# A merged attention and delta-rule stage: moved reductions, one more copy on ScalarE, doubled output buffers, and a mask that becomes a limit

## The reference

```python
# head group A, per block of 128 queries
s = einsum(qn, k_nope) + einsum(qp, k_pe)          # scaled
s = where(k_pos <= q_pos, s, -inf)
o = softmax(s) @ v
# head group B, per chunk and head (g is the cumulated log decay of the chunk)
decay = exp(where(causal, g[:, None] - g[None, :], -inf))
lower = where(strict, (k_beta @ k.T) * decay, 0)
sol   = triangular_solve(lower + eye, [v_beta, k_beta * exp(g)])
a_qk  = where(causal, (q @ k.T) * decay, 0)
# then a scan over chunks that carries a state of 128 x 128 per head
```

## Time and profile before

| | |
|---|---|
| median of 3 runs | 2444.69 us (2444.61 to 2447.8) |
| the profiled execution | 2443.78 us |
| its span | 2442.0 us |
| TensorE busy, whole span | 2187.7 us |
| VectorE, ScalarE, GpSimd busy, whole span | 1028.3, 839.1, 652.5 us |
| merged stage, first instruction of TensorE | 691.58 us |
| output stage, first of TensorE | 1502.00 us |

### The profile page before, as it was taken

The page is one execution under the profiler, slowest core; times in us unless marked ns, Lnnn a source line. Parts: engine busy times, 40 slices in busy tenths (PEclk is TensorE's granted clock), DMA queues, the critical chain, the costliest instruction groups (busy, mean ns, idle before and its releaser), DMA issues. The chain is left out here.

```text
span 2442.0 us, 35600 instructions
## 1 busy us (share of the span) xinstructions
PE 2187.7 (90%) x11479; PEld 1242.1 (51%) x11480; DVE 1028.3 (42%) x2282; ACT 839.1 (34%) x2043; POOL 652.5 (27%) x1122
## 2 busy tenths in 40 slices
PE   5999999999967898899889996999948999999990
PEld 2545455545434565666656673455534444444440
DVE  2334243333345576666677663243451222222223
ACT  2264363552644454454544551111111111111113
POOL 1000001000034534624633501333322222222224
PEclk9999999999988999999999997999968999999995
DMA  9212121121252333434244218533305888999777
GB/s 344 80 61 76 48 76 57 45 76 61 85 171 78 111 122 121 146 107 139 77 135 143 70 53 316 185 123 131 112 26 154 225 246 267 303 324 294 220 220 299
DMA packets 221897, 361.77 MB, mean 148 GB/s; under 512 B 45579, under 2 KB 143526, under 8 KB 218294
## 3 DMA queue, kind: packets, MB, share of 16 engines
q1 hardware_dynamic: 207926, 309.57, 37.2%
q0 software_dynamic: 13824, 50.34, 8.6%
HBM read 259.93 MB, written 99.93 MB: 147 GB/s over the span
## 5 line engine op out<-in xcount | busy, mean ns | idle before, releaser
L704 PE MATMUL pV<-keys_values_then_all,w_in_sb 128*128 128x512 f32 x768 | 341.5, 598 | 4.1 <-DVE keys_values_then_all L518 4.1
L2170 PE MATMUL hidden_ps<-w,keys_values_then_all 128*128 x752 | 332.5, 595 | 1.7 <-SPq L2042 1.7
L1234 ACT ACTIVATE probs<-scores,neg_max 128x512 f32<-128x512 f32 (+3 forms) x320 | 196.3, 620 | 302.4 <-DVE neg_max L1343 182.1
L2170 PEld LDWEIGHTS hidden_ps<-w,keys_values_then_all 128*128 128x128 f32 x752 | 143.5, 191 | 182.8 <-issue 182.8
L704 PEld LDWEIGHTS pV<-keys_values_then_all,w_in_sb 128*128 128x128 f32 x768 | 145.0, 191 | 177.8 <-issue 177.0
L1808 PE MATMUL out_ps<-keys_values_then_all 128*128 128x512 f32 x512 | 226.8, 601 | 2.8 <-ACT keys_values_then_all L1657 2.8
L1496 PE MATMUL scores<-ident,probs 128*128 128x128 f32 x1088 | 155.9, 285 | 39.8 <-ACT probs L1234 39.1
L2100 ACT ACTIVATE keys_values_then_all<-hidden_ps 128x256 f32<-128x256 f32 x47 | 18.0, 383 | 457.0 <-PE hidden_ps L2170 457.0
L2180 PE MATMUL expert_ps<-w_sb,keys_values_then_all 128*128 x368 | 169.8, 604 | 0.0
L1808 PEld LDWEIGHTS out_ps<-keys_values_then_all 128*128 128x128 f32 x512 | 97.1, 192 | 122.5 <-issue 116.7
L1496 PEld LDWEIGHTS scores<-ident,probs 128*128 128x128 f32 x1088 | 120.3, 143 | 69.7 <-ACT probs L1234 60.9
(11 more groups left out here) (370 smaller groups left out, 3310.3 us busy)
## 6 DMA issues: line engine op xcount, KB each, us to landing
w<-in_w_dram SPq DMA_DIRECT2D x64, 1024.0 KB, 10.2
w_sb<-in_w_dram SPq DMA_DIRECT2D x32, 1024.0 KB, 14.2
keys_values_then_all<-in_x_dram SPq DMA_DIRECT2D x32, 512.0 KB, 5.4
w_mod_rows<-in_w_mod_dram SPq DMA_DIRECT2D x16, 1024.0 KB, 4.9
keys_values_then_all<-in_w_mod_dram SPq DMA_DIRECT2D x4, 2048.0 KB, 14.9
qkv_d<-l_out SPq DMA_DIRECT2D x32, 256.0 KB, 2.3
keys_values_then_all<-y_d SPq DMA_DIRECT2D x16, 512.0 KB, 4.7
x_d<-keys_values_then_all SPq DMA_DIRECT2D x16, 512.0 KB, 2.8
```

Of the source, the lines that this page charges most:

```text
L704: last = pe.matmul(pV[n % 2][:], win[:, k, QKV0 + c * P:QKV0 + (c + 1) * P], hT[:, s % 2, k, :], start=(k == 0), stop=(k == ND - 1))
L1234: act.activation(prob[:, e, 0:w].rearrange("p t k -> p (t k)"), pS[e][:, 0:w * P], ACT.Exp, scale=-1.0, bias=nmin[:, i % 2, h, b:b + 1], a ...
L2170: last = pe.matmul(pH[par][:], xT[par][:, k], m.w13[:, ds(slot, 1), k].rearrange("p s n -> p (s n)"), start=(k == 0), stop=(k == ND - 1))
```

## The change

- `X j+1` of heads 2 and 3 is put directly behind those of heads 0 and 1, behind the scores and ahead of `V j`; before, they stood between the halves of `V j`.
- The transposed probabilities of head 1 are copied by ScalarE too: three copies there, one on VectorE.
- One of the two `O` turns of a quad goes behind `V`.
- `A` comes at the end of the second quad of a tile in every case, and `AS` behind the minima of the tile's last quad, or, where the tile before has fewer than four key tiles, in the next tile's first quad; the last ones are put by hand.
- `G` and `O2` are held back until the next `V`, or until the next `K` or `QS`.
- GpSimd's multiplication by the triangle is gone. Instead VectorE's `G` is a subtraction followed by a minimum with a tile `future` (zero in the triangle, -1e30 outside), and `K` and `KA` read the exponential straight from `dm`.
- `A_ahead` and `qk_ahead` have two buffers each, by the parity of the chunk.
- SyncE loads the next decay rows behind the stores of `KA` in place of behind `K`, and several loads of the stage's start (keys and queries, gate, bias, modulation weights) go behind the first stores.

```diff
-        if i and o < AH // 4:
-            for hp in (2 * o, 2 * o + 1):
-                atoms.append((0.13 * (TILE[i - 1] // 4 + 1), [("O", i - 1, hp)]))
+        if i > 1 and first and TILE[i - 1] < 4:
+            atoms.append((0.0, [("AS", i - 2, 0)]))
+        turns = [(0.13 * (TILE[i - 1] // 4 + 1), [("O", i - 1, hp)]) for hp in (2 * o, 2 * o + 1)] * (i > 0 and o < AH // 4)
+        atoms += turns[:1]
         if ahead:
-            atoms.append((0.8 * ahead, [("S", j + 1), ("X", j + 1, 0), ("X", j + 1, 1)]))
-        if i and last:
-            atoms.append((0.0, [("A", i - 1, 0)] * (TILE[i] < 4) + [("AS", i - 1, 0)]))
-        atoms.append((0.65 * n, [("V", j, 0)] + [("X", j + 1, 2), ("X", j + 1, 3)] * (ahead > 0) + [("V", j, 1)]))
-        if i and o == AH // 4 - 1 and TILE[i] >= 4:
+            atoms.append((0.8 * ahead, [("S", j + 1)] + [("X", j + 1, e) for e in range(4)]))
+        if i and last and TILE[i] >= 4:
+            atoms.append((0.0, [("AS", i - 1, 0)]))
+        atoms.append((0.65 * n, [("V", j, 0), ("V", j, 1)]))
+        atoms += turns[1:]
+        if i and o == AH // 4 - 1:
             atoms.append((0.0, [("A", i - 1, 0)]))
...
-    atoms.append((0.0, [("BX", NT - 1, 0), ("B2", NT - 1, 0)]))
+    atoms.append((0.0, [("AS", NT - 2, 0), ("BX", NT - 1, 0), ("B2", NT - 1, 0)]))
...
+    held = []
     for cost, step in steps:
+        if step[0] in ("O2", "G"):
+            held.append(step)
+            continue
+        if step[0] in ("K", "QS"):
+            order += held
+            held = []
         order.append(step)
         owed += cost * share
         while atoms and owed >= atoms[0][0]:
             owed -= atoms[0][0]
-            order += atoms.pop(0)[1]
+            order += atoms[0][1]
+            if atoms.pop(0)[1][0][0] == "V":
+                order += held
+                held = []
+    order += held
...
@@ sync
-            load_kk(2)
-            load_q(1)
-            load_gate(0)
-            ...
-            load_mod(0)
+            def load_next():
+                ...   # the same loads
...
-                    if n + 2 < NT:
-                        wait(em_ready, n + 1)
-                        load_g(n + 2)
                 elif kind == "KA":
                     store_products(n)
+                    if n + 2 < NT:
+                        load_g(n + 2)
+                    if n == 0:
+                        load_next()
...
@@ gpsimd
+            pool.memset(future[:], 0.0).then_inc(limit_made, 1)
+            pool.wait_ge(limit_made, 1)
+            pool.affine_select(out=future[:], in_=future[:], compare_op=ALU.is_ge, fill=NEG, base=0,
+                               pattern=[[1, P]], channel_multiplier=-1).then_inc(limit_made, 1)
...
-                if kind == "G":
-                    wait(exp_ready, n + 1)
-                    wait(at_ready, n)
-                    pool.tensor_tensor(em[:], dm[:, n % 2], m.upper[:].unsqueeze(1).to_broadcast([P, GH, P]), ALU.mult).then_inc(em_ready, 1)
...
@@ scalar
-                elif kind == "T" and step[2] % 2 == 0:
+                elif kind == "T" and step[2] < 3:
...
@@ vector
-                        last = dve.tensor_scalar(dm[:, n % 2, h], dm[:, n % 2, h], gcol[:, cols(n, h)], 0.0, ALU.subtract, ALU.min)
+                        last = dve.scalar_tensor_tensor(out=dm[:, n % 2, h], in0=dm[:, n % 2, h], scalar=gcol[:, cols(n, h)], in1=future[:],
+                                                        op0=ALU.subtract, op1=ALU.min)
...
-                    wait(em_ready, n + 1)
-                    wait(lt_stored, 16 * n)
+                    wait(decay_ready, n + 1)
+                    wait(lt_stored, 16 * (n - 1))
...
-                    wait(at_stored, 16 * n)
+                    wait(at_stored, 16 * (n - 1))
...
-                elif kind == "T" and step[2] % 2 == 1:
+                elif kind == "T" and step[2] == 3:
...
@@ tensor, S and V
-                    for half in range(2):
-                        wait(t_copied[half], 2 * n)
+                    wait(t_copied[0], 3 * n)
+                    wait(t_copied[1], n)
...
-                    for e in range(2):
-                        wait(t_copied[e], u + 1)
+                    wait(t_copied[0], 3 * n + 2 + step[2])
+                    wait(t_copied[1], n + step[2])
```

More of the change, by code:

```diff
@@ L868, in mix @@
         gates = sb("gate_in", [P, 2, GH, GD])
-        dm, em = sb("g_rows_then_decay", [P, 2, GH, P]), sb("decay", [P, GH, P])
-        lt, lt_new, at_new = (sb(n, [P, GH, P]) for n in ("A_transposed", "A_ahead", "qk_ahead"))
+        dm, future = sb("g_rows_then_decay", [P, 2, GH, P]), sb("decay_limit", [P, P])
+        lt = sb("A_transposed", [P, GH, P])
+        lt_new, at_new = sb("A_ahead", [P, 2, GH, P]), sb("qk_ahead", [P, 2, GH, P])
         corner = m.kv[QK:P, CORNER:CORNER + 4096]
@@ L982, in store_products @@
                 wait(lt_ready, c + 1)
[L983 removed]
+                sp.dma_start(m.a_d[c * P:(c + 1) * P, :], lt_new[:, c % 2].rearrange("p h i -> p (h i)")).then_inc(lt_stored, 16)
                 wait(at_ready, c + 1)
[L985 removed]
+                sp.dma_start(m.qk_d[c * P:(c + 1) * P, :], at_new[:, c % 2].rearrange("p h i -> p (h i)")).then_inc(at_stored, 16)
             def load_blocks(c):
@@ L1046, in _ @@
             load_g(1)
-            load_kk(2)
-            load_q(1)
-            load_gate(0)
-            sp.wait_ge(bias_zero, 1)
-            for r in range(8):
-                sp.dma_start(mod_sum[32 * (r % 4):32 * (r % 4) + 1, r // 4], b_mod[0:1, 2 * D + r * 512:2 * D + (r + 1) * 512]).then_inc(bias_loaded, 16)
-            load_mod(0)
+            def load_next():
+                load_kk(2)
+                load_q(1)
+                load_gate(0)
+                sp.wait_ge(bias_zero, 1)
+                for r in range(8):
+                    sp.dma_start(mod_sum[32 * (r % 4):32 * (r % 4) + 1, r // 4], b_mod[0:1, 2 * D + r * 512:2 * D + (r + 1) * 512]
+                                 ).then_inc(bias_loaded, 16)
+                load_mod(0)
             sp.wait_ge(mask_made, 1)
@@ L1120, in _ @@
                                pattern=[[-1, P]], channel_multiplier=1).then_inc(mask_made, 1)
-            done, made = [0], {"G": 0, "O1": 0, "A": 0}
+            done, made = [0], {"O1": 0, "A": 0}
             def then(ins):
@@ L1130, in invert @@
                 n = P - QK
-                wait(em_ready, made["G"])
                 wait(o_pow, 2 * made["O1"])
@@ L1193, in _ @@
                     wait(dm_ready, n + 1)
-                    act.activation(dm[:, n % 2], dm[:, n % 2], ACT.Exp).then_inc(exp_ready, 1)
+                    act.activation(dm[:, n % 2], dm[:, n % 2], ACT.Exp).then_inc(decay_ready, 1)
                 elif kind == "VT":
@@ L1260, in _ @@
             wait = waiter(dve)
+            dve.wait_ge(limit_made, 2)
             dve.wait_ge(mask_made, 2)
@@ L1270, in _ @@
                     wait(kk_ready, n + 1)
-                    wait(em_ready, n + 1)
-                    wait(lt_stored, 16 * n)
+                    wait(decay_ready, n + 1)
+                    wait(lt_stored, 16 * (n - 1))
                     both = [bank[b] for b in at_bank[step]]
                     for h in range(GH):
-                        last = dve.scalar_tensor_tensor(out=lt_new[:, h], in0=both[h // 2][:, (h % 2) * 2], scalar=beta[:, cols(n, h)],
-                                                        in1=em[:, h], op0=ALU.mult, op1=ALU.mult)
+                        last = dve.scalar_tensor_tensor(out=lt_new[:, n % 2, h], in0=both[h // 2][:, (h % 2) * 2], scalar=beta[:, cols(n, h)],
+                                                        in1=dm[:, n % 2, h], op0=ALU.mult, op1=ALU.mult)
                     last.then_inc(lt_ready, 1)
                 elif kind == "KA":
-                    wait(at_stored, 16 * n)
+                    wait(at_stored, 16 * (n - 1))
                     both = [bank[b] for b in at_bank[("K", n)]]
                     for g in range(2):
-                        last = dve.tensor_tensor(at_new[:, g * 2:g * 2 + 2], both[g][:].rearrange("p (h two) i -> p h two i", two=2)[:, :, 1],
-                                                 em[:, g * 2:g * 2 + 2], ALU.mult)
+                        last = dve.tensor_tensor(at_new[:, n % 2, g * 2:g * 2 + 2], both[g][:].rearrange("p (h two) i -> p h two i", two=2)[:, :, 1],
+                                                 dm[:, n % 2, g * 2:g * 2 + 2], ALU.mult)
                     last.then_inc(at_ready, 1)
```

4 lines of the change are left out of this document (2 added, 2 removed).

## The result

The changed kernel took 2413.43 us (median of 4 runs, 2410.43 to 2419.23) against 2444.65 before; the ratio is 0.9876, with a 95% interval of 0.9854 to 0.9898. That is 31 us less where 38.6 were forecast, and inside the range. The profiled execution of the changed kernel is the slowest of its four, 2419.23, so its trace shows 24.5 us of the gain.

What follows compares the result with a forecast made beforehand. TensorE, busy 90% of the span, was taken as the bound, with 88.5 us idle in the stage's window to win from. Terms 6.2 + 10 + 10 + 0 + 5 - 6 + 5 - 1.6 + 10 = 38.6 gave 2406 us; eight-in-ten range 2390 to 2432.

Steps and rivals of the forecast that it cites:

- The start: Stage start: second K waits for no store, later loads, triangle off GpSimd; second scores earlier, 6.2 us won [4.8 to 7.2].
- AS and A: ScalarE: all four exponentials now ahead of AS, so its wait for GpSimd's root holds less; 10 of 13.1 us won.
- the O turns: VectorE's O work spread over two places cuts TensorE's 14.5 us of bank waits; 5 us won [0 to 9].
- The triangle: Multiplication leaves GpSimd, so K no longer waits for it late; 10 of 12.2 us won [6 to 12.2].
- `G` and `O2` held: VectorE: slower two-tensor G stands behind V, competing with head 3's copy alone; taken 0 us [-12 to 0].
- The minima: All four minima behind the scores: cuts the transposes' remaining 12.9 us of waits; 5 us won [0 to 8].
- Three copies: 80 copies go from VectorE to ScalarE; with one O turn fewer before scores, later score waits rise: -6 us [-20 to 0].
- the rival with ScalarE last: Scores wait for ScalarE's three copies in every quad, each 0.54 us later: 2453 us; chance 0.06.
- The end: Stage end: tile 14's last O turn goes behind V 79, so A and AS start one turn later: -1.6 us [-2 to 0].
- The clock: Fewer long TensorE waits, so fewer low-clock stretches behind them; 10 of 18.9 us won [5 to 17].
- the waits move: Rival: TensorE's waits move to the next late thing instead of vanishing; half the sum, 2425 us; chance 0.20.
- The other sign against me: Waits of 3 us on a root or a bank take the place of those on exponentials.

Runs made afterwards that it cites:

- the fastest kernel of all: Changed kernel with two copies per engine, nothing held back, A one quad later, last tile's O turns, A and AS as before: 2391.09 us, ratio 0.9783.

## Why the prediction was right, and where its terms were off

The direction, the size and the main mechanism hold: the waits on the exponentials went, 39.1 to 4.6 us, and with the minima apart again 20.0 us of them came back. The net was 31 where 38.6 were summed. That it came so close is in part luck. The triangle is worth 37 to 39 us in this order, where 10 were summed, and two parts that were costed at nothing or at little, the held steps and the third copy, take 9 to 13 and 8 to 11 us. These are effects of undoing one part each; they depend on each other and do not add up to the net. Term by term:

- *The start, 6.2.* The second scores came 5.9 us sooner in the stage. The buffers and loads are 3.4 of it, of which I had 5.0, and 0 to 4 us of the whole; the triangle is 1.6, of which I had 1.2; some 0.9 is left over, which no run isolates.
- *AS and A, 10, and the O turns, 5 with a loss inside the 6.* Undone together they made no difference that can be told. The long waits behind `AS` did go: ScalarE's waits for the root fell from 11.6 us (longest 5.3) to 5.2 (3.4). But the `O` turn that was moved behind `V` makes the sum that `A` reads, and it now stands directly ahead of `A`; ScalarE waits for that sum ahead of the copies (13.6 us in ten waits). I had costed the turn for the scores and the banks, and had not asked which step reads its result next. That is the first step that failed; moved a quad on, `A` gives 14 to 16 us where three copies stand behind it, and 2 to 3 with two.
- *The triangle, 10.* In an order with nothing held it is worth 13 to 16. In the order of the change it is worth 37 to 39, since held steps put the multiplication just ahead of its reader. So without this edit the change would have been slower than the kernel before (1.0027). Some 11 of the 35 us that the stage is longer without it are TensorE's own work at a lower clock.
- *`G` and `O2` held, costed at nothing.* The second failure: holding costs 9 to 13 us. I had named the cover, the idle time of VectorE behind `V`. But a step held until `K` is run in a row with `O2` and `K` ahead of the last copy or of an `O` turn, and the clock falls behind the waits that this makes. By the traces idle time is 6.0 us of it and busy time 8.1. The price of `G` itself was right: its mean went from 328 to 472 ns, 64 x 0.144 = 9.2 us of VectorE's time, inside the 4.5 to 11.8 given. The Trainium skill, page "VectorE: DVE Perf Modes", section "Mode 2×_2P — use both read ports for one tensor", says that fp32 runs at twice the rate with one SBUF tensor and not with two. The medians agree in direction, 279 against 348 ns, a ratio of 1.25 for the whole instruction; that is 4.4 us for 64, and the mean is more, as some of them took up to 847 ns. (The 342 ns that the prediction set beside the 279 are of an operation that reads a bank in PSUM; 348 is the fair one.)
- *The minima, 5.* 9 to 11 in place, 15 alone: under-sized. That it gives more alone is presumably because it then takes over what the moves of `AS` and the triangle would give; no run parts these.
- *Three copies, -6 with the O turns.* -8 to -11, and not for the reason given. The rival with ScalarE last was right about the place and wrong about the cause: the copies wait for `A`, and with `A` moved the third copy costs nothing that can be told.
- *The end, -1.6.* -4.6 in the traces. The turn was counted; that the last `A` has to wait for the store of the `AS` before it, so that an `AS` 2.6 us later behind the last `V` makes the whole end later, was not.
- *The clock, 10.* In the two traces next to nothing: summed over windows of 10 and 20 us, the stretch of the earlier trace rows loses some 25 us of full clock before and after alike. The stretch at the lower level behind the start's wait went, but new ones stand behind waits of 2.6 to 3.6 us, as at 900 and 950. But the traced execution of the changed kernel is the one of its four with the lowest clock: a mean of 0.956 over its span, where the others have 0.958 or 0.959; the traced one of the kernel before has 0.958, where 38 executions of it beside the experiments have 0.9555 in the mean. The missing share of the clock times the span is then 109 us before and 101 after, over all executions, each good to about 1 us, as the clock is given in three digits. By this estimate some 7 or 8 of the 10 us came. It moves with the waits in the other kernels as well: 122 us with the triangle back on GpSimd, 90 in the fastest kernel of all. So a good part of what an order of steps is worth here comes back through the clock.

Of the rivals, "the waits move" was the truest account of what kept the gain down, in the copies; its time, 2425, is further off than the forecast's.

The marks given beforehand: no wait above 3 us on an exponential, and their total under 20, held (4.6, longest 2.8). The scores' waits, 17 to 30 forecast, were 37.8; of the 40 for ScalarE's copies that I had named as proof against me, 24.3 came. The other sign against me, waits of 3 us on a bank, showed in two places: 3.00 us at 952.78, and 4.49 us at 1462.68, at the end, where a wait of 3.71 stood before. Over the whole span VectorE is 40.5 us less busy, as forecast, and ScalarE 33.0 more, not 43: copies in a row overlap, so that 80 more of them, at a mean of 537 ns, add 31.8 us of busy time. The output stage's first matmul came 24 us earlier in the trace, not 38. The windows under 0.8 of the clock after 730 did not go.

## What to carry to other kernels

When a step is moved in a list that every engine walks, ask at its new place what it waits for itself, what then stands behind it on its engine, and which step reads its result next. The moved `O` turn ahead of `A`, and the held steps, took back a good part of what the other moves gave. A small step on a busy in-order queue between a producer and a reader (here 1.3 us of GpSimd behind pieces of inversion) is worth its lateness, not its duration, and the closer the producer is put to the reader the dearer it gets (13 to 16 us and 37 to 39 here). Undo the parts of a bundle one at a time, and then in pairs: two parts of this one were losses where they stood, and one of these was no loss any more once `A` stood elsewhere. Without both, with `A` a quad later and the old end, the kernel runs in 0.9783 of the time of before in place of 0.9876. Compare clocks over all executions, not over one trace of each kernel.

## What was not expected of the hardware

- Two-tensor operations on VectorE with both inputs in SBUF ran from 335 to 847 ns for the same 128x128 shape (L1286 in the changed kernel); four in a row took 1.13 us at 1302.87, where GpSimd did nothing, and 2.69 us at 742.96, where it was in the inversion.
- In the two kernels with the triangle back on GpSimd, the twelve waits of `K` that the profile puts down to "issue" each ended within 0.5 us of the end of GpSimd's multiplication; only the timeline shows it. "issue" does not mean that nothing was waited for.
- Waits of much the same length did not cost the same clock. The 10 us from 900 in the changed kernel, whose longest wait is 2.57 us, have a granted clock of 0.66, between its levels of 2.4 and 1.2 GHz; the 10 us from 1000, just behind a wait of 2.79 us, have 0.84.
